# Two early seven-product pairs among the row blocks, and the sums of h behind the last block, in a transformer block on one Trainium2 core

## The reference

```python
x = x + rmsnorm(m @ w_out[l], g_post_mix[l])
h = rmsnorm(x, g_pre_ffn[l])
g, u = jnp.split(h @ w_gate_up[l], 2, axis=-1)
x = x + rmsnorm((jax.nn.silu(g) * u) @ w_down[l], g_post_ffn[l])
```

## Time and profile before

| what | value |
|---|---|
| median of three runs | 745.42 us (744.99 to 745.82) |
| the profiled execution's own time | 746.07 us |
| its span in the profile | 744.2 us |
| PE busy | 736.8 us (99%), 4305 matmuls |
| DVE busy | 577.1 us (78%) |
| ACT busy | 443.6 us (60%) |
| POOL busy | 258.0 us (35%) |
| granted TensorE clock over the span | 0.998 |

### The profile page before, as it was taken

How to read it: one execution, slowest core, us unless ns; L and a number is a source line. 1 busy time by engine, 2 the same in 40 slices (tenths; PEclk the granted TensorE clock), 3 DMA queues, 4 the chain that set the end, 5 groups by cost and what they waited for, 6 DMA issues and landing times.

```text
span 744.2 us, 11986 instructions
## 1 busy us (share of the span) xinstructions
PE 736.8 (99%) x4305; PEld 651.2 (88%) x4305; DVE 577.1 (78%) x826; ACT 443.6 (60%) x713; POOL 258.0 (35%) x204
## 2 busy tenths in 40 slices
PE   9999999999999999999999999999999999999997
PEld 7788888888888888888888999999999999788885
DVE  4979989977656656348998887777887776985787
ACT  5763177777758676753575754555555554765564
POOL 5837265975777869321004300000000000034101
PEclk9999999999999999999999999999999999999999
DMA  9662444222304224179970033333333334999904
GB/s 333 184 179 63 147 117 114 57 58 61 109 11 126 65 70 114 57 201 290 256 196 5 1 114 114 113 102 85 95 113 113 113 113 156 339 189 205 211 16 114
DMA packets 111521, 95.23 MB, mean 128 GB/s; under 512 B 3696, under 2 KB 91768, under 8 KB 111480
## 3 DMA queue, kind: packets, MB, share of 16 engines
q1 hardware_dynamic: 104920, 78.96, 34.4%
q0 software_dynamic: 6368, 15.73, 11.5%
q10 hardware_dynamic: 192, 0.01, 0.0%
HBM read 84.97 MB, written 4.73 MB: 121 GB/s over the span
## 4 chain that ended last, share of the span: by engine, by line
PE 94%; DVE 2%; ACT 1%; issue 1%; DMA 1%; POOL 0%; POOLq 0%; SPq 0%; DVEq 0%; ACTq 0%
PE ps L1084 11%; PE ps L688 11%; PE ps L690 11%; PE ps L689 11%; PE ps L1019 9%; PE ps L1021 9%; PE ps L1020 9%; PE ps L709 6%; PE ps L951 4%; PE ps L750 3%; PE ps L908 3%; PE ps L897 2%; PE ps L971 1%; PE ps L880 1%; PE ps L882 1%
## 5 line engine op out<-in xcount | busy, mean ns | idle before, releaser
L688 PE MATMUL ps<-h_hi,w_hi 128*128 128x512 f32 (+1 forms) x288 | 111.1, 386 | 0.0
L690 PE MATMUL ps<-h_hi,w_lo 128*128 128x512 f32 (+1 forms) x288 | 109.3, 380 | 0.0
L689 PE MATMUL ps<-h_lo,w_hi 128*128 128x512 f32 (+1 forms) x288 | 109.2, 379 | 0.0
L1859 POOL DMA_DIRECT2D w_a<-in_w_down x12 | 15.3, 1532 | 253.3 <-DVE xd_lo L2410 246.9
L1773 POOL TENSOR_TENSOR w_lo<-raw,w_hi 128x1024 fp32r<-128x1024 f32 x30 | 78.2, 2610 | 30.5 <-ACT w_hi L1280 30.1
L1019 PE MATMUL ps<-t_hi,sum_hi 128*128 128x256 f32 x240 | 67.9, 283 | 0.0
L1020 PE MATMUL ps<-t_lo,sum_hi 128*128 128x256 f32 x240 | 67.9, 283 | 0.0
L1021 PE MATMUL ps<-t_hi,sum_lo 128*128 128x256 f32 x240 | 67.9, 283 | 0.0
L690 PEld LDWEIGHTS ps<-h_hi,w_lo 128*128 128x128 f32 x288 | 54.1, 188 | 10.2
L2405 DVE TENSOR_TENSOR wr_lo<-w_a,wr_hi 128x1536 fp32r<-128x1536 f32 (+1 forms) x28 | 45.4, 1623 | 21.6 <-ACT wr_hi L1582 21.6
L688 PEld LDWEIGHTS ps<-h_hi,w_hi 128*128 128x128 f32 x288 | 54.3, 188 | 8.6
(11 more groups left out here) (341 smaller groups left out, 2187.3 us busy)
## 6 DMA issues: line engine op xcount, KB each, us to landing
raw<-in_w_in SPq DMA_DIRECT2D x40, 512.0 KB, 4.5
raw<-in_w_gate_up SPq DMA_DIRECT2D x24, 512.0 KB, 3.9
raw<-in_w_gate_up SPq DMA_DIRECT2D x40, 256.0 KB, 4.3
w_a<-in_w_down SPq DMA_DIRECT2D x9, 768.0 KB, 7.0
w_a<-in_w_down POOLq DMA_DIRECT2D x9, 768.0 KB, 10.0
s<-in_w_out SPq DMA_DIRECT2D x3, 768.0 KB, 8.1
...
```

The lines of the kernel that those rows point to most:

```text
L688: mm(acc, whi_c, a_hi_, start=first, stop=False)
L689: mm(acc, whi_c, a_lo_, start=False, stop=False)
L690: return mm(acc, wlo_c, a_hi_, start=False, stop=last)
```

## The change

`PLAIN` becomes 1 and `SEVENS` 21. Pairs 0 and 1 of the seven-product kind ("early") have products 1 and 2, which need only the first token half, among the row blocks, where the second plain pair's tiles were. As bank halves are shared, two matmuls with zeros first clear banks 2 and 3, and all that accumulates there does so without a start flag. The sums of h come right behind the last block, in the order 0, 2, 1, 3, with `early` made in two parts; the products that need them are written out, the two pairs interleaved. The early pairs have buffers of their own; their weight sums stay on POOL, which also takes one rest; the sums of pair 2 are made by VectorE ahead of the loop. SP loads pair 0 in place of the second plain pair, and pair 2 when `parts_lo_done` reaches `REST_0`. In the loops `window` now comes before `finish_pair`, one pair later.

TensorE:

```diff
-        for i in range(4):
-            first_part(T_UP, i, 0, 2)
-            if i in (1, 2):
-                turn(i + 1, y_buf)
-        for i in range(4):
-            first_part(T_UP, i, 2, 4)
...
+        for b in (2, 3):
+            ins = mm(bank(b), zeros[:, :], early_hi[0][:, 0:512], start=True, stop=True)
+        ins.then_inc(product_done, 1)
+        early_product(0, 1)
+        first_part(T_UP, 0, 0, 2)
+        parts_made(EARLY_1)
+        pe.wait_ge(product_kept, KEPT_1[0])
+        early_product(1, 1)
+        turn(2, y_buf)
+        first_part(T_UP, 1, 0, 2)
+        turn(3, y_buf)
+        pe.wait_ge(product_kept, KEPT_1[1])
+        early_product(0, 2)
+        early_product(1, 2)
+        for i in range(2):
+            first_part(T_UP, i, 2, 4)
+        parts_made(SUMS_0)
+        pe.wait_ge(t_done, T_LOW[0])
+
+        mm(bank(5, HALF), h_hi[:, 0, 0:P], h_hi[:, 0, 0:HALF], start=True, stop=True)
+        early_product(0, 5)
+        pe.wait_ge(t_done, T_LOW[2])
+        early_product(0, 6)
+        parts_made(SUMS_1)
+        early_product(1, 5)
+        parts_made(REST_0)
+        pe.wait_ge(t_done, T_LOW[1])
+        pe.wait_ge(product_kept, KEPT_6[0])
+        early_product(0, 7)
+        early_product(0, 3)
+
+        pe.wait_ge(silu_done, PLAIN + 1)
+        early_product(1, 6)
+        pe.wait_ge(t_done, T_LOW[3])
+        pe.wait_ge(summed_up, UP_2[0])
+        early_product(0, 4)
+        parts_made(REST_1)
+        pe.wait_ge(product_kept, KEPT_6[1])
+        early_product(1, 7)
+        early_product(1, 3)
+        pe.wait_ge(summed_up, UP_2[1])
+        early_product(1, 4)
...
-        mm(bank(5, HALF), h_hi[:, 0, 0:P], h_hi[:, 0, 0:HALF], start=True, stop=True).then_inc(product_done, 1)
-        seven(0, 0, lambda n: pe.wait_ge(t_done, OUT_T + 5 + n))
-        pe.wait_ge(act_done, 2 + PLAIN)
-        mm(bank(1, HALF), h_hi[:, 0, 0:P], h_hi[:, 0, 0:HALF], start=True, stop=True)
+        pe.wait_ge(silu_done, PLAIN + 3)
         with pe.Fori(0, SEVENS // 2 - 1) as j:
             for v in (1, 0):
-                seven(j * 2 + (2 - v), v)
+                seven(j * 2 + (3 - v), v)
```

VectorE, from the last norm on (`early_sums_rest(p, n)` takes the rest of 1024 columns of pair p's sums, `last_quarter_rest(p)` of 512):

```diff
+        ve.wait_ge(parts_hi_done, SUMS_0)
+        ve.wait_ge(parts_lo_done, EARLY_1)
+        early_sums_rest(0, 0).then_inc(parts_lo_done, 1)
         second_norm(3)
         rest_turned(2)
...
+        rest_turned(3)
+        ve.wait_ge(parts_hi_done, REST_0)
+        early_sums_rest(0, 1)
+        ve.wait_ge(early_made, 1)
         ve.wait_ge(t_hi_done, 1)
         tt(t_plain(0), early[:, 0:KC // 2, :], late[:, :, :], sub).then_inc(t_done, 1)
-        tt(in_blocks(t_plain(1)), late_down, in_blocks(late[:, :, :]), sub).then_inc(t_done, 1)
...
+            ve.wait_ge(t_done, OUT_T + 4)
...
+        t_rest(0)
+        t_rest(2)
+        early_sums_rest(1, 0).then_inc(parts_lo_done, 1)
+        t_rest(1)
+        last_quarter_rest(0).then_inc(parts_lo_done, 1)
+        ve.wait_ge(silu_done, 1)
+        ve.wait_ge(tile_done, T_UP + 2)
+        ve.wait_ge(parts_lo_done, SUMS_1)
+        tt(act[:, 0, :], silu[:, 0, :], bank(1), ALU.mult).then_inc(act_done, 1)
+        t_rest(3)
+        ve.wait_ge(parts_hi_done, REST_1)
+        early_sums_rest(1, 1)
+        last_quarter_rest(1).then_inc(parts_lo_done, 1)
...
+        early_up_2(0)
+        early_gate_two(0)
+        raw_sums(2, 1)
+        second_sum(2, 1)
+        third_sum(2, 1)
+        early_finish(0)
+        early_up_2(1)
+        quarters_rest(2, 1)
+        sums_rest(2, 1, 0)
+        early_gate_two(1)
+        early_finish(1)
+        sums_rest(2, 1, 1)
         with ve.Fori(0, SEVENS // 2 - 1) as j:
             for v in (1, 0):
-                finish_pair(j * 2 + (1 - v), 1 - v)
-                window(j * 2 + (2 - v), v)
+                window(j * 2 + (3 - v), v)
+                finish_pair(j * 2 + (3 - v), v)
```

ScalarE:

```diff
-        for u in range(2):
-            run(wu_hi[:, u, :], raw[:, (T_UP + 2 + u) % 4, :], ACT.Copy).then_inc(w_hi_done, 1)
+        early_hi_of(0)
...
         first_norm(0)
+        early_hi_of(1)
...
         round_turned(0)
+        sc.wait_ge(product_done, OUT_PRODUCTS)
+        early_sums_hi(0, 0).then_inc(parts_hi_done, 1)
         round_turned(1)
+        early_sums_hi(0, 1)
         first_norm(3)
         second_norm(2)
-        sc.wait_ge(y_normed, TB)
-        quarters_hi(0, 0)
+        early_first_kept(0)
+        early_sums_hi(1, 0).then_inc(parts_hi_done, 1)
+        last_quarter_hi(0).then_inc(parts_hi_done, 1)
         second_norm(3)
+        early_first_kept(1)
...
+        early_fifth_kept(0)
+        early_sums_hi(1, 1)
+        last_quarter_hi(1).then_inc(parts_hi_done, 1)
+        early_sixth_kept(0)
+
+        sc.wait_ge(product_done, ended[0, 6])
+        early_silu(0)
+        early_fifth_kept(1)
+        early_silu_two(0)
+        sc.wait_ge(product_done, ended[0, 3])
+        early_sixth_kept(1)
+        quarters_hi(2, 1)
+        sc.wait_ge(product_done, ended[0, 4])
+        early_silu(1)
+        sums_hi(2, 1, 0)
+        sums_hi(2, 1, 1)
+        early_silu_two(1)
```

POOL and SP:

```diff
+        gp.wait_ge(y_normed, 1)
+        first_sums(0)
+        gp.wait_ge(x_normed, 1)
+        last_sums(0)
+        gp.wait_ge(x_normed, 2)
+        gp.wait_ge(parts_hi_done, EARLY_1)
+        gp.wait_ge(parts_lo_done, low[S4])
+        nc.gpsimd.tensor_tensor(early_lo[1][:, :], raw[:, 0, :], early_hi[1][:, :], sub).then_inc(parts_lo_done, 1)
+        first_sums(1)
+        gp.wait_ge(h_lo_done, 2)
+        gp.wait_ge(block_done, TB)
+        early_values(0)
+        gp.wait_ge(x_normed, 3)
+        last_sums(1)
+        gp.wait_ge(x_normed, TB)
+        early_values(1)
...
         for p in range(2):
-            sp.wait_ge(w_lo_done, T_DOWN - 2 + 2 * p)
...
+            sp.wait_ge(w_lo_done, T_UP + 2 * p)
+            sp.wait_ge(up_in, p * 48 + OUT_IN)
+            quarters(p, 1 - p)
         for p in range(2, SEVENS):
             sp.wait_ge(up_in, p * 48 + OUT_IN)
+            if p == 2:
+                sp.wait_ge(parts_lo_done, REST_0)
             raw_free(p - 1)
```

More of the change, by code:

```diff
@@ L43 @@
 Q = KC // 2 * P
-SEVENS = FC - 2
+SEVENS = FC - 1
 W = HEADS * HD
@@ L226, in build @@
     ends = sb("ends", TRI)
-    top[0] = zone1
     top[0] = zone1 + 4 * KC * D
-    wu_hi, wu_lo = sb("wu_hi", [2, D], F32R), sb("wu_lo", [2, D], F32R)
+    early_hi, early_lo = [], []
+    for p in range(2):
+        early_hi.append(sb(f"early_hi{p}", 2 * Q, F32R))
+        early_lo.append(sb(f"early_lo{p}", 2 * Q, F32R))
     top[0] = zone1
@@ L459, in build @@
         OUT_PARTS + 3 * SEVENS, 4 * SEVENS, OUT_PRODUCTS + 7 * SEVENS + 1, OUT_KEPT + 3 * SEVENS, OUT_SUMMED + 2 * SEVENS + 4)
+    order = [(0, 1), (1, 1), (0, 2), (1, 2), (0, 5), (0, 6), (1, 5), (0, 7), (0, 3), (1, 6), (0, 4), (1, 7), (1, 3), (1, 4)]
+    ended = {which: OUT_PRODUCTS + 2 + n for n, which in enumerate(order)}
+    KEPT_1, KEPT_5, KEPT_6 = ([OUT_KEPT + n for n in two] for two in ((1, 2), (3, 5), (4, 6)))
+    UP_2, GATE_2 = ([OUT_SUMMED + 4 + n for n in two] for two in ((1, 3), (2, 4)))
+    T_LOW = {i: OUT_T + 5 + n for n, i in enumerate((0, 2, 1, 3))}
     plain = {A11: s_11, A12: s_12, S2: s_two, S3: s_11, A22: s_22, S1: s_one, S4: s_12,
@@ L486, in x_plain @@
         return group_of(t2n, g) if k == 4 else act_group(*{0: (0, 0), 1: (1, 0), 3: (0, 1), 6: (1, 1)}[k], g)
+    early_m = [bank(2 + p, HALF) for p in range(2)]
+    early_gate = [ps[:, 3 - p, HALF:S] for p in range(2)]
+    early_c = [bank(7 - p, HALF) for p in range(2)]
     block = ctx.enter_context(nc.Block())
@@ L618, in _ @@
         sp.dma_start(g_ffn_row[:, :], g_pre_ffn[0:1, :].partition_broadcast(P)).then_inc(g_ffn_in, 16)
-        for j in range(1, PLAIN):
-            pair(T_UP // 2 + j, j, cols(wup, 0, P, FF))
         def quarters(p, v):
@@ L1029, in t_sum, with early_product @@
             return t_hi[:, i, :, :], t_lo[:, i, :, :]
-        def seven(p, v, t_rest=None):
+        def early_product(p, n):
+            quarter, part, last = ((hi[p], lo[p]) for hi, lo in ((early_hi, early_lo), (part_hi, part_lo), (a22_hi, a22_lo)))
+            m, gate, c = early_m[p], early_gate[p], early_c[p]
+            acc, (hi, lo), col, by, first = {
+                1: (m, quarter, 0, h_quarter(0, 0), False), 2: (gate, quarter, Q, h_quarter(1, 0), False),
+                5: (c, part, 0, t_sum(0), True), 6: (m, part, Q, t_sum(2), False), 7: (m, part, 2 * Q, t_sum(1), False),
+                3: (c, part, 3 * Q, h_quarter(1, 1), False), 4: (m, last, 0, t_sum(3), False)}[n]
+            product(acc, hi, lo, col, *by, first).then_inc(product_done, 1)
@@ L1482, in sums_hi, with early_sums_hi, last_quarter_hi, early_first_kept @@
             sc.wait_ge(sum_made, p * 4 + (n + 3))
-            run(sum_hi[v][:, 2 * Q * n:2 * Q * (n + 1)], sums_of(p, v, 2 * n, 2), ACT.Copy).then_inc(parts_hi_done, 1)
+            part = slice(2 * Q * n, 2 * Q * (n + 1))
+            run(sum_hi[v][:, part], sums[v][:, part], ACT.Copy).then_inc(parts_hi_done, 1)
```

(34 more changed lines are left out.)

222 lines of the change are left out of this document (107 added, 115 removed).

## The result

The changed kernel takes **748.07 us** (median of 7 runs, 747.45 to 749.12) against 745.42 (7 runs, 744.99 to 746.35): a ratio of 1.003, interval 1.0020 to 1.0039, so 2.65 us slower. Forecast were 747.85, a range of 745.2 to 749.8 and a slower kernel. The profiled execution of after took 747.45, its span is 745.7.

What follows compares the result with a forecast made beforehand. TensorE, busy 99%, was taken to set the end while other engines keep ahead. A gain of 1.11 less stalls of 1.18 and about 2.36 made +2.43 us on 745.42: 747.85, range 745.2 to 749.8.

Steps and rivals of the forecast that it cites:

- The gain, 1.11: TensorE up to the first looped pair: 12 matmuls (1.44) and a dummy (0.12) saved, less zeroing (0.45); at most 1.11 us.
- The last turn and the covers costed at nothing: Row blocks: slack hides changed loads, rounding and POOL overlap; the last turn keeps 0.2 to 1 us; cost nothing.
- Before 405 TensorE waits for nothing: Run up to 405 us, ahead of the edited stretch: TensorE has no waits there, so edits there were costed at nothing.
- The first stall, 1.18: First product needing h's chunk sums: TensorE ready at 424.72, VectorE's t_lo lets it go at 425.90; 1.18 us lost.
- The second limit, VectorE's queue: First looped pair, product 4: VectorE's queued work delays up_2, so it starts at 451.42, not 449.06; about 2.36 us.
- the +2.0 that the prediction gives for a shorter one: Pair 2's weights: if 1 MB lands after 4.4 us and not 4.9, the total change would be +2.0 us.
- the silu's round trip: Finishing pair 1: VectorE waits for ScalarE's silu (0.04 + 0.42 + 0.27), idle 0.73 us.
- ScalarE's late copies: First looped pair: stop TensorE 0.7 us at product 6, 1 us at product 7; covered by VectorE's lateness, 0.6 to spare.
- nothing more is lost: From the second looped pair on: VectorE starts its sums 0.65 us after TensorE's pair, as before, so no further cost.
- The signs: Expected evidence: TensorE share below 99%, t_lo wait 1.0 to 1.4 us, first looped pair's waits 0.5 to 2.5, longest for silu.
- The queue packs tighter: Rival, VectorE's queue: its and the DMA's waits (0.8, 0.73) partly vanish; +0.8 to +1.4, about 746.5 us; chance 0.22.
- VectorE keeps up: Rival: t_lo by 424.7 and looped pair's up_2 by 447.9, so only the matmul saving counts; 744.3 us; chance 0.09.

Runs made afterwards that it cites:

- e10: e8 with two more small VectorE operations, gate_two of pair 0 and up_2 of pair 1, each moved ahead of a long one; 744.75 us against 745.84 before.
- e2: Changed kernel with 1.74 us of VectorE rests moved into its idle gap before the last block's rest, pair 2's weights issued earlier; 748.29 us against 745.59 before.
- e3: e2 with pair 2's sums ahead of pair 0's up_2, its rests spread between small operations, ScalarE's roundings moved ahead likewise; 746.65 us against 745.59 before.
- e1: Changed kernel with the rest of the first chunk sum of h (t_lo 0) made before the fourth sum; 747.88 us against 745.59 before.
- e5: e3 with POOL's second half of early ahead of its last sums, and those behind the first chunk sum; 746.04 us against 745.79 before.
- e6: e5 with e1's earlier t_lo 0 and the early pairs' products in another order on TensorE; 746.40 us against 745.79 before.
- e8: e6 with up_2 of pair 0 moved between the first two and last two sums of pair 2 on VectorE; 745.94 us against 746.18 before.
- e4: Changed kernel with e3's VectorE order alone; weights, gap and ScalarE's order as they were; 753.27 us against 745.59 before.

## Why the prediction was right, point by point

**The gain, 1.11.** Right. In all ten kernels with the change, late starts less 1.11 give the distance within 0.08, and e10, nearly without waits, is 0.70 shorter by the sum and 0.72 by the rows.

**The last turn and the covers costed at nothing.** The matmul behind the last turn comes 10.74 us after the start in after, as in before plus the zeroing (10.29 + 0.45). The overlap with POOL that the prediction named is there (the rest at 410.29 takes 1.41, `y_buf` behind it 1.81), 0.2 and 0.5 longer than their usual 1.22 and 1.28, and stays within the slack. In e2 and e3, too, the last turn keeps its place (10.74 us after the start); what comes late there is the last block's `h_lo`, behind a rest that these kernels put beside POOL. "Before 405 TensorE waits for nothing" is a misreading: the kernel before has waits of 1.1 and 0.3 us in its first 5 us, but after has the first of them too (1.07), and the sum does not use it.

**The first stall, 1.18.** Its place was right: `t_lo` lets TensorE start 20.74 us after the blocks' start, forecast 20.63. It cost 1.38: TensorE goes about 0.15 us after `t_lo` is done and not 0.05, and the slower matmul behind a wait (0.08) was missing from the sum. Wrong was to let it stand as a term of the sum beside the second: e1 takes 0.53 of it away and the time stays. The forecast came out right because the second term was worked out as VectorE's absolute time, into which the first stall doesn't enter.

**The second limit, VectorE's queue.** Product 4 of the first looped pair starts 46.16 us after the blocks' start (450.86 - 404.70); the forecast was 46.15 (451.42 - 405.27). That they agree to 0.01 is luck, for errors inside cancelled. Pair 2's sums start 0.35 later than forecast (29.93 against 29.58; the wait for the weights is 1.19, not 0.8). The transfer itself was as forecast (the +2.0 that the prediction gives for a shorter one is +1.9 by its own sum): its data moved until 434.3, 4.9 us after the issue at 429.38; missing was the time from there until VectorE goes on, at 434.63:

```profile
434.20:434.30 0.10, 0.10 (x3) 0.10 (x3) 0.00 (x0) 0.00 (x0) 0.00 (x0) 1.00 0.11 26
```

On the other side the silu's round trip leaves 0.48 of idle time rather than 0.73, and the last two rests before `up_2` take 2.27 from start to start (448.12 to 450.39), not 2.38. ScalarE's late copies were named as stopping TensorE at products 6 and 7 (0.7 and 1 us); they cost 0.60 and 0.75, and VectorE's lateness covered them by 0.40, not 0.6 (product 4 could otherwise have started at 450.46). A wait for ScalarE's `sum_hi` at the looped pair's first product (0.42) was not forecast. Like the two others it is covered.

**The whole.** For the stretch +2.53 against a forecast of +2.43: the missing 0.10 is product 4 itself, 1.53 us long after its wait rather than 1.44. Behind it the forecast had nothing, "nothing more is lost"; the rows have 0.48 won at the last pair, where before had the wait of the earlier trace rows. The reading of that row had seen a wait without asking where it stands. So by the rows the change costs 2.05, and that the medians' 2.65 lies only 0.22 from the forecast is luck in part. The range, 745.2 to 749.8, began below the kernel before and was wide enough for most of the rivals.

**The signs.** The wait at the first `t_lo`, VectorE's one long wait, for the weights, and the spacing of 0.12 elsewhere came as named. Two signs did not come. The page's share of TensorE stayed at 99% (736.5 of 745.7). And the first looped pair's waits are 0.16 to 0.49 us, the longest for ScalarE's `u`, where 0.5 to 2.5 and the longest for `silu` were named: the second stall is 2.33 in all, against 2.36, but in four pieces at products 1, 6, 7 and 4 (0.42, 0.60, 0.75, 0.50), with 0.06 ahead of the pair.

**The rivals.** "The queue packs tighter" did not happen in the changed kernel, and it was the one with most in it: the idle times were not work, and e3, e5, e6 and e8 to e10 remove them by the order and the earlier transfer. "VectorE keeps up" named the right condition, `up_2` of the looped pair 3.5 us ahead of the list, 42.6 us after the blocks' start. In e10 it starts at 447.84 - 405.40 = 42.44 and is done at 42.85, 0.2 after that; TensorE, 0.38 late itself by the first `t_lo`, does not ask for it before 43.01, and the gain is there but for that `t_lo`. The argument against it, that all durations in the list are rows, was the weak one: the durations were right, and the order was free.

```profile
447.84 0.41 DVE L2488 TENSOR_TENSOR silu<-ps,p_kept 128x256 f32<-128x256 f32 x1
```

**What stays open.** How much of e3's 1.60 over e2 is VectorE's order and how much ScalarE's was not separated: e4, meant for it, was swamped by the late weights. Whether e10's last 0.31 at `t_lo` can be had was not tried; 0.12 of it may be POOL again, whose last sum ends at 423.93, while this `t_lo` (423.68) takes 1.34 rather than 1.22. How the change takes away the wait at the last pair was not tested.
